# FFN tails of three down tiles by token tile, and low weight halves made behind the softmax, in a float32 two-block transformer on one core

## What is computed

```
def swiglu_2(h, w_in, w_out):
    gate, up = jnp.split(h @ w_in, 2, axis=-1)
    return (jax.nn.silu(gate) * up) @ w_out

for i in range(4):                       # block 2
    x = x + 0.5 * rms_norm(swiglu_2(rms_norm(x, g[0]), ffn_w_in[i, 0], ffn_w_out[i, 0]), g[1])
    m = (A, B, C, A)[i](rms_norm(x, g[2]))
    x = x + rms_norm(m, g[3])
    x = x + 0.5 * rms_norm(swiglu_2(rms_norm(x, g[4]), ffn_w_in[i, 1], ffn_w_out[i, 1]), g[5])
```

## Time and profile before

| | |
|---|---|
| median of 3 runs | 2722.29 us (2721.77 to 2724.02) |
| profiled execution, its own time | 2723.01 us |
| its span | 2721.2 us |
| mean granted PE clock | 0.989 |
| PE busy | 2608.3 us (96%), 15276 matmuls |
| PE weight loads | 2250.0 us (83%) |
| DVE busy | 1822.5 us (67%) |
| ACT busy | 1476.5 us (54%) |
| POOL busy | 196.6 us (7%) |
| DMA | 465.43 MB, mean 171 GB/s |
| chain that ended last | PE 80%, DVE 7%, ACT 6%, issue 2%, DMA 2% |

### The profile page before, as it was taken

The page is one execution under the profiler, slowest core; times in us unless marked ns, Lnnn a source line. Parts: engine busy times, 40 slices in busy tenths (PEclk is TensorE's granted clock), DMA queues, the critical chain, the costliest instruction groups (busy, mean ns, idle before and its releaser), DMA issues.

```text
span 2721.2 us, 43395 instructions
## 1 busy us (share of the span) xinstructions
PE 2608.3 (96%) x15276; PEld 2250.0 (83%) x15276; DVE 1822.5 (67%) x2531; ACT 1476.5 (54%) x2373; POOL 196.6 (7%) x271
## 2 busy tenths in 40 slices
PE   7999998999999989999989999999999999999999
PEld 6888887888888868888878688888888888887887
DVE  5766667666676676666677566666656667666766
ACT  4655547455555565455555654554556556455644
POOL 0200002000000030000001200000110000003000
PEclk9899999999999999999999999999999999999999
DMA  4448844567566436656654266566446665643564
GB/s 148 140 157 223 219 124 131 170 200 217 170 193 193 141 117 208 186 170 203 190 174 136 86 185 185 170 201 192 139 137 192 190 201 173 190 155 126 178 190 142
DMA packets 581742, 465.43 MB, mean 171 GB/s; under 512 B 19524, under 2 KB 542340, under 8 KB 581124
## 3 DMA queue, kind: packets, MB, share of 16 engines
q1 hardware_dynamic: 579300, 456.10, 55.6%
q0 software_dynamic: 1696, 7.40, 1.1%
q10 hardware_dynamic: 640, 0.52, 0.1%
HBM read 460.76 MB, written 4.25 MB: 171 GB/s over the span
## 4 chain that ended last, share of the span: by engine, by line
PE 80%; DVE 7%; ACT 6%; issue 2%; DVEq 2%; DMA 2%; POOL 1%; SPq 0%; ACTq 0%; POOLq 0%
PE acc L714 20%; PE tp L699 14%; PE gu L699 13%; PE tp L703 8%; PE gu L703 7%; PE gu L681 3%; DVE lo_a L448 2%; ACT hi_a L436 2%; PE acc L1339 1%; PE acc L1341 1%; PE acc L1340 1%; PE tp L1212 1%; DVE x L661 1%; PE gu L1308 1%; PE gu L1300 1%
## 5 line engine op out<-in xcount | busy, mean ns | idle before, releaser
L448 DVE TENSOR_TENSOR lo_a<-raw_a,hi_a 128x2048 fp32r<-128x2048 f32 (+1 forms) x313 | 711.1, 2272 | 364.4 <-ACT hi_a L436 362.7
L436 ACT ACTIVATE hi_a<-raw_a 128x2048 fp32r<-128x2048 f32 (+1 forms) x313 | 590.9, 1888 | 103.1 <-PE acc L1341 27.5
L699 PE MATMUL tp<-xT,hi_a 128*128 128x512 f32 x1760 | 439.9, 392 | 0.0
L699 PE MATMUL gu<-xT,hi_a 128*128 128x512 f32 x1600 | 397.9, 391 | 0.0
L699 PEld LDWEIGHTS tp<-xT,hi_a 128*128 128x128 f32 x1760 | 323.3, 189 | 62.3
L699 PEld LDWEIGHTS gu<-xT,hi_a 128*128 128x128 f32 x1600 | 294.1, 188 | 56.9
L714 PE MATMUL acc<-hi_b,h_hi 128*128 128x512 f32 x800 | 314.1, 393 | 0.4 <-DVE h_lo L806 0.4
L714 PE MATMUL acc<-lo_b,h_hi 128*128 128x512 f32 x800 | 313.7, 392 | 0.0
L714 PE MATMUL acc<-hi_b,h_lo 128*128 128x512 f32 x800 | 311.2, 389 | 0.0
L459 DVE TENSOR_TENSOR lo_b<-raw_b,hi_b 128x1024 fp32r<-128x1024 f32 x220 | 268.1, 1219 | 21.8 <-ACT hi_b L455 21.8
L774 ACT ACTIVATE arena<-arena 128x256 f32<-128x256 f32 x220 | 92.0, 418 | 319.8 <-DVE arena L795 319.8
(11 more groups left out here) (299 smaller groups left out, 3762.0 us busy)
## 6 DMA issues: line engine op xcount, KB each, us to landing
raw_a<-in_ffn_w_in SPq DMA_DIRECT2D x352, 512.0 KB, 5.7
raw_b<-in_ffn_w_out SPq DMA_DIRECT2D x176, 512.0 KB, 3.6
raw_a<-in_w_in SPq DMA_DIRECT2D x52, 512.0 KB, 4.7
raw_a<-in_w_gate SPq DMA_DIRECT2D x44, 512.0 KB, 5.7
raw_a<-in_w_up SPq DMA_DIRECT2D x44, 512.0 KB, 6.8
raw_b<-in_w_down SPq DMA_DIRECT2D x44, 512.0 KB, 4.5
raw_a<-in_w_out SPq DMA_DIRECT2D x24, 512.0 KB, 4.3
raw_a<-in_c_w_in SPq DMA_DIRECT2D x24, 512.0 KB, 4.6
```

What stands on the lines that cost most here:

```text
L436: nc.scalar.activation(a_view(hi_a, par)[:, :, 0:width], a_view(raw_a, par)[:, :, 0:width], ACT.Copy).then_inc(a_hi, 1)
L448: nc.vector.tensor_tensor(a_view(lo_a, par)[:, :, 0:width], a_view(raw_a, par)[:, :, 0:width], a_view(hi_a, par)[:, :, 0:width].bitcast(F3 ...
L699: nc.tensor.matmul(banks[:, e, :], w_hi[:, kt, e * P:(e + 1) * P], xT[:, :, kt, :], start=(kt == 0), stop=False)
```

## The change

Three edits.

**FFN, tail.** The last input tile is made by `last_in_pe`, with 256-column products that all go into `tp[:, e, 0:256]`, so that ACT has no part to copy and DVE none to add; `gate_part` is gone. It stands on PE right behind input tile FT-2, ahead of down tile FT-3. `ffn_last_pe` then does three down tiles (FT-3, FT-2, FT-1), token tile 0 first. The third keeps its halves in `oT_hi` and `oT_lo` (`h_hi3`, `h_lo3`, `b_hi3`, `b_lo3`). ACT makes the first high slot of the next stage between the Silu and the last high half (`ffn_last_act`), DVE its low half behind the last `h_lo` (`ffn_last_dve`).

**A and C.** In the odd steps the low half of the next slot is made behind values and softmax, ahead of `rden_dve`.

**B.** In odd steps from p = 27 on, the low half is made at the end of the step (this concerns p = 27, 29, 37, 41 and 47).

```diff
+        b_hi3, b_lo3 = (v[:, 0:4, :].rearrange("p k t -> p (k t)") for v in (oT_hi, oT_lo))
+        h_hi3, h_lo3 = oT_hi[:, 4, :], oT_lo[:, 4, :]
...
+        def last_in_pe(pe, s):
+            n, m = s.a0 + FT - 1, s.b0 + FT - 1
+            pe.wait_ge(a_hi, n + 1)
+            pe.wait_ge(hid_ready, m - 1)
+            w_hi, w_lo = a_view(hi_a, n), a_view(lo_a, n)
+            for e in range(2):
+                o, half = tp[:, e, 0:256], slice(e * P, (e + 1) * P)
+                for kt in range(KT):
+                    nc.tensor.matmul(o, w_hi[:, kt, half], xT_hi[:, kt, :], start=(kt == 0), stop=False)
+                    nc.tensor.matmul(o, w_hi[:, kt, half], xT_lo[:, kt, :], start=False, stop=False)
+                if e == 0:
+                    pe.wait_ge(a_lo, n + 1)
+                for kt in range(KT):
+                    mm = nc.tensor.matmul(o, w_lo[:, kt, half], xT_hi[:, kt, :], start=False, stop=(kt == KT - 1))
+                mm.then_inc(a_used if e else gate_done, 1)
...
             ffn_in_pe(pe, s, s.a0 + FT - 2, s.b0 + FT - 2, s.a0 % 2, 0)
-            ffn_out_pe(pe, s.b0 + FT - 3, 1)
-            ffn_in_pe(pe, s, s.a0 + FT - 1, s.b0 + FT - 1, (s.a0 + 1) % 2, 1, last=True)
+            last_in_pe(pe, s)
             ffn_last_pe(pe, s)
...
-            for t, c in ((0, 0), (0, 1), (1, 0)):
-                bank_pe(0, t, c, False)
-            pe.wait_ge(hid_lo, m + 2)
-            pe.wait_ge(b_lo, m + 2)
+            for j in range(2):
+                tile_ready(j)
+                for c in range(2):
+                    bank_pe(j, 0, c)
+            tile_ready(2)
             for c in range(2):
-                bank_pe(1, 0, c, True).then_inc(out_done, 1)
-            bank_pe(0, 1, 1, False).then_inc(b_used, 1)
-            bank_pe(1, 1, 0, True).then_inc(out_done, 1)
-            bank_pe(1, 1, 1, True).then_inc(b_used, 1)
+                bank_pe(2, 0, c).then_inc(out_done, 1)
+            for j in range(3):
+                mm = bank_pe(j, 1, 0)
+            mm.then_inc(out_done, 1)
+            for j in range(3):
+                bank_pe(j, 1, 1).then_inc(b_used, 1)
...
+        def ffn_last_act(act, n, m, more_a):
+            act.wait_ge(hid_scaled, m + 1)
+            nc.scalar.activation(sg[:, 1, :], gs[:, 1, :], ACT.Silu).then_inc(hid_gate, 1)
+            if more_a:
+                hi_slot_a(act, n + 1)
+            act.wait_ge(hid_ready, m + 1)
+            nc.scalar.activation(h_hi3, hh32[:, 1, :], ACT.Copy).then_inc(hid_hi, 1)
+            if more_a:
+                hi_slot_a(act, n + 2)
...
+        def ffn_last_dve(dve, n, m, more_a):
+            dve.wait_ge(gate_done, m // FT + 1)
+            nc.vector.tensor_tensor(gs[:, 1, :], tp[:, 0, 0:256], rb, ALU.mult).then_inc(hid_scaled, 1)
+            lo_slot_b(dve, m, 1, True)
+            dve.wait_ge(a_used, n + 1)
+            dve.wait_ge(hid_gate, m + 1)
+            dve.wait_ge(hid_lo, m - 1)
+            dve.wait_ge(hid_hi, m - 1)
+            nc.vector.tensor_tensor(hh32[:, 1, :], sg[:, 1, :], tp[:, 1, 0:256], ALU.mult).then_inc(hid_ready, 1)
+            dve.wait_ge(hid_hi, m + 1)
+            nc.vector.tensor_tensor(h_lo3, hh32[:, 1, :], h_hi3.bitcast(F32), ALU.subtract).then_inc(hid_lo, 1)
+            if more_a:
+                lo_slot_a(dve, n + 1)
...
-                    if h == 1:
-                        ahead_a(lo_slot_a, dve, s.a0 + i + 1)
                     if scored(s, p - 3) is not None:
                         values_dve(dve, s, scored(s, p - 3))
                     if scored(s, p) is not None:
                         woven_soft_dve(dve, s, scored(s, p))
+                    if h == 1:
+                        ahead_a(lo_slot_a, dve, s.a0 + i + 1)
...
-                ahead_b(lo_slot_a, dve, s, p)
+                if p % 2 == 0 or p < 27:
+                    ahead_b(lo_slot_a, dve, s, p)
...
+                if p % 2 and p >= 27:
+                    ahead_b(lo_slot_a, dve, s, p)
```

More of the change, by code:

```diff
@@ L683, in first_products, with ffn_in_pe @@
             return mm
-        def ffn_in_pe(pe, s, n, m, pa, pm, first=False, last=False):
+        def ffn_in_pe(pe, s, n, m, pa, pm, first=False):
             pe.wait_ge(a_hi, n + 1)
@@ L742, in bank_pe @@
+            def bank_pe(j, t, c):
+                l_hi, l_lo, r_hi, r_lo = tiles[j]
                 w = slice(c * 512, (c + 1) * 512)
-                for i, (l, r) in enumerate(((h_hi, hi_b), (h_hi, lo_b), (h_lo, hi_b))):
-                    mm = nc.tensor.matmul(acc[:, 2 * t + c, :], l[:, pm, t * P:(t + 1) * P], r[:, pm, w],
-                                          start=False, stop=(stop and i == 2))
-                return mm
-            m = s.b0 + FT - 2
-            pe.wait_ge(hid_lo, m + 1)
@@ L750, in ffn_last_pe @@
[L750 to L766 removed]
+                for i, (l, r) in enumerate(((l_hi, r_hi), (l_hi, r_lo), (l_lo, r_hi))):
+                    mm = nc.tensor.matmul(acc[:, 2 * t + c, :], l[:, t * P:(t + 1) * P], r[:, w], start=False, stop=(j == 2 and i == 2))
@@ L807, in ffn_tile_dve, with ffn_tiles, pair @@
                 .then_inc(hid_lo, 1)
-            if more_a == "ahead":
-                lo_slot_a(dve, n + 1, par=1 - pa)
-            elif more_a and more_b:
+            if not tail:
                 lo_slot_a(dve, n + 2, par=pa)
-            if more_b:
                 lo_slot_b(dve, m + 1, 1 - pm)
-        def ffn_tiles(eng, s, tile, ends=(True, True)):
-            def pair(i, more_a, end):
+        def ffn_last_dve(dve, n, m, more_a):
[11 more added lines that the diff above has]
+                lo_slot_a(dve, n + 1)
+        def ffn_tiles(eng, s, tile, last):
+            def pair(i):
                 for e in range(2):
-                    tile(eng, 2 * i + (s.a0 + e), 2 * i + (s.b0 + e), (s.a0 + e) % 2, e, more_a[e], not (end and e))
-            pair(0, (True, True), False)
+                    tile(eng, 2 * i + (s.a0 + e), 2 * i + (s.b0 + e), (s.a0 + e) % 2, e, False, s.b0 // FT)
+            pair(0)
             with eng.Fori(1, FT // 2 - 1) as i:
-                pair(i, (True, True), False)
-            pair(FT // 2 - 1, ends if s.a0 + FT < A_TOTAL else (False, False), True)
+                pair(i)
+            tile(eng, s.a0 + FT - 2, s.b0 + FT - 2, s.a0 % 2, 0, True, s.b0 // FT)
+            last(eng, s.a0 + FT - 1, s.b0 + FT - 1, s.a0 + FT < A_TOTAL)
         def ffn_act(act, s):
```

51 lines of the change are left out of this document (22 added, 29 removed).

## The result

| | before | changed |
|---|---|---|
| median, us | 2724.02 (5 runs) | 2739.87 (5 runs, 2736.43 to 2743.36) |
| ratio of the runs | | 1.0061, 95% interval 1.0046 to 1.0076 |
| profiled execution's span | 2721.2 | 2741.5 |
| granted PE clock | 0.989 | 0.983 |

What follows compares the result with a forecast made beforehand. Time is lost where PE (96% busy) waits. FFNs -10.4, A +11.6, C +7.2, B -1.0 and clock +3.4 sum to +10.8 us on the profiled 2723.0; with the median 0.7 lower, 2733.0 us, range 2721 to 2740.

Steps and rivals of the forecast that it cites:

- The FFN sum: All FFNs: -5.0 us for ten tails and -5.4 behind eight of them, together -10.4 (-4 to -12).
- -0.68 behind it: After an FFN tail: token tile 0 finishes earlier, so token tile 1's chain runs alone, 0.68 us sooner.
- low weights and softmax make a chain that an output step cannot cover: A stage: scores, softmax and low half take 6.3 us, PE covers 3.1, so an output step waits 3.2 us.
- its 0.4 for a DVE that is free earlier: A stage: 0.4 us saved behind the last matmul, making +6.2 into +5.8 a stage, +11.6 for two.
- In C the stalls: C stage: waits at low slots 3, 6, 9 and transposes, then slots 12 and 13; +7.2 us (+4 to +8.5).
- B's -1.0: B stage: earlier softmax at p=37 and POOL freed by slot 15's move; -1.0 us (-2.4 to 0).
- rival (a): A and C: POOL's slowdown binds and low slots come in time; 2700 us, chance 0.04; slots partly late, 2714, 0.06.
- The step that failed: Clock term: five new waits in A and C each cost 0 or 1.7 us; two taken, +3.4 (0 to +8.5).
- The rival that the clock falls in all five waits: Second half of rival (c), new waits in A and C: +16 us; chance 0.15 shared with a late third down tile.
- the one counterexample of before: A stage of the kernel before: around a 2.9 us PE wait the granted clock stayed at 1.00.

Runs made afterwards that it cites:

- the kernel with step 7 alone: Changed kernel, but C ordered as before and in A only step 7's low slot made behind the softmax; 2707.05 us, ratio 0.9938; run again 2710.09 us.
- the kernel with the mixers' edits alone: Kernel before plus the change's edits of A, B and C, with the old FFN tails; 2751.08 us, ratio 1.0100.
- the FFN tails alone: Changed kernel with A, B and C put back in the order of before, only the new FFN tails kept; 2718.06 us, ratio 0.9976.
- The version with filled ends: The kernel with step 7 alone, plus unread PE transposes in the waits for x at stage ends; 2703.83 us, ratio 0.9930; run again 2704.59 us.

## Why the prediction was right in sign and a third short

**Right, by their rows.** The FFN sum was forecast at -10.4 us, from -0.5 a tail (-0.55 and -0.48 measured in block 1, where nothing else is in it) and -0.68 behind it (3.71 to 3.04). The prediction names seven FFNs that another stage follows and counts eight tails; the last FFN is 1.1 us shorter too. That low weights and softmax make a chain that an output step cannot cover was forecast wait by wait. As stalls between two starts, beyond the pitch, in the first A stage:

| place | forecast | measured |
|---|---|---|
| low slot 3 | 0.9 | 0.90 |
| transposes of units 0 and 1 | 0.5, 0.6 | 0.57, 0.66 |
| low slot 5 | 4.1 | 3.95 |
| low slot 6 | 3.8 | 3.65 |
| low slots 7 and 8 | 1.7, 1.8 | 1.51, 1.72 |

Sum 13.4 forecast, 13.0 measured, and 0.40 at a place that I had at nothing. Against the stalls of before (3.07, 0.73, 1.23, 0.42, 1.72) that is +6.2, the number that the prediction had before its 0.4 for a DVE that is free earlier. This 0.4 came behind the last matmul (1.36 us between starts became 1.01), but the wait for token tile 1 at the start of the stage grew by as much (1.64 to 2.04). In C the stalls are 0.96 and 0.73 three times (1.0 and 0.8 forecast), and 2.93 and 1.14 for slots 12 and 13 (+1.9 and +1.2 forecast, +1.9 and +1.14 measured). B's -1.0 is -1.2. POOL's multiplies take 1.61 us as foretold, and rival (a) falls with the waits shown: taking POOL's slowdown away at step 7 is worth 2.0 us at that wait and 0.6 to 1.2 us a stage (the kernel with step 7 alone), and the slots do not come in time.

**The step that failed** is the clock: "Each can cost 0 or 1.7; I take two, **+3.4**". Both factors were too small. The stretch up to the second set of output matmuls takes 3.21 us at full clock (969.12 to 972.33 before) and 5.90 behind slot 5, 5.89 behind slot 6 now: 2.7 us each, not 1.7. The 1.7 came from one stretch of 3.4 us in B, and the same profile has stretches of 6.8 and 10.2 us at 1.2 GHz in its hybrid stages that I did not price. And it was not two waits of five but all four in A, and the one in C, behind which the clock is low from 2044 on. In A that makes some 5.4 and 4.5 us. In C it is 1.6: from the first to the second output slot (2043.17 to 2053.83) PE takes 10.66 us, and 9.06 in the kernel with the mixers' edits alone, where the clock stays up there. So the term was 3.4 in the sum and is 11.5 in the profiled execution, which was 3.5 us slower than the median of its runs.

The stages add up with it. First A: 6.2 + 5.4 + 1.3 for the low clock behind its start = 12.9, measured +13.0. C: its order costs 7.4 (128.45 us in the kernel with the mixers' edits alone, 121.04 with the FFN tails alone, neither with a low stretch), of which 6.7 are stalls; 1.6 come by the clock, and about 1 goes, because C began with a low stretch before (from 1940.7) and does not now. That is +8.0, measured +8.1. In the first 13 us of block 2's stages there are five low stretches before and five now, the one of A and the one of C just named among them.

The rival that the clock falls in all five waits was there, at +16 together with another at a chance of 0.15; it was what happened in the profiled execution, and it had the price of 1.7 in it as well. I let the one counterexample of before, a wait of 2.9 us without a drop, speak for the odds. The kernel with the FFN tails alone shows what that example was worth: the same wait (2.92 and 2.95 us), with a drop behind it in both A stages.

That idle time of PE is what lets the clock fall is shown (slot 5's wait filled in two A stages of one profile, the waits for x at 11 starts in each of two more; no drop behind any of them). What decides whether a given wait of 1.8 to 4 us is followed by it was not found out.

## What to carry to other kernels

Price a wait of PE like these at its length plus the work behind it at half speed: here 0.8 to 2.7 us on top of waits of 1.8 to 3.9, where the clock fell. Take that from the longest such stretch of the trace, and do not take a wait without one as proof. Before a producer is moved behind other work, look for the step where it is needed before anything else can run: of the slots moved in A and C, two of A cost as much as the net loss, those of C cost 7.4 us together, and one of A was worth its move. And where a wait can't be had away, idle matmuls in it may be cheaper than the clock behind it.

## What was not expected of the hardware

- 32 idle transposes in a 3.95 us wait of PE, in an otherwise unchanged program, take away the 2.7 us that the next 22 matmuls would have lost.
- A wait of 1.77 us (before token tile 1 of the FFN at 2236) is followed by a clock of 0.72 over 6 us; filled, at the same place, by 1.00. That a wait this short can be enough was new. It is not always: of the seven starts with this wait three were followed by a drop in one profile and two in the other of the same kernel.
- One kernel's runs differ in it: the changed kernel's five lie between 2736.4 and 2743.4, the fastest with a mean granted clock of 0.987 and the slowest with 0.983. The version with filled ends lies between 2703.0 and 2705.4, and between 2703.2 and 2707.7 when run again; that it spreads less because of the filling is not shown.
